# Token sums of squares ahead of four feed-forwards: one 512-column product of a high and a low part in place of a float32 product

## The chip, the cores and the metric

The kernel runs on one core of one Trainium2 chip. The metric is the device time of one launch in microseconds (us), and the reported number is the median of several runs. Before the change it is 1018.36 us (three runs, 1017.70 to 1018.63).

Engines are named as the profile names them: PE is TensorE (PEld its weight loads), DVE is VectorE, ACT is ScalarE, POOL is GpSimd, SP is SyncE, which only starts DMAs here.

## The reference

The input x is 256 tokens by 1024 features in float32, and the trunk has two layers. Each layer is feed-forward, mixer, feed-forward, with a root-mean-square norm ahead of every part:

```
def rms_norm(x, g):
    xf = x.astype(jnp.float32)
    y = xf * lax.rsqrt(jnp.mean(xf * xf, axis=-1, keepdims=True) + NORM_EPS)
    return (y * g.astype(jnp.float32)).astype(x.dtype)

def swiglu(h, w_in, w_out):
    gate, up = jnp.split(h @ w_in, 2, axis=-1)
    return (jax.nn.silu(gate) * up) @ w_out

for i in range(DEPTH):                       # DEPTH = 2
    x = x + 0.5 * swiglu(rms_norm(x, ffn1_norm[i]), ffn1_w_in[i], ffn1_w_out[i])
    hm = rms_norm(x, mix_norm[i])
    # layer 0: retention; layer 1: sliding-window attention over one shared K/V
    x = x + mixer(hm)
    x = x + 0.5 * swiglu(rms_norm(x, ffn2_norm[i]), ffn2_w_in[i], ffn2_w_out[i])
    if i == 0:
        k_sh, v_sh = shared_kv(x, kv_norm, kv_w, k_norm)
```

There are six norms of x, numbered m = 0 to 5: feed-forward, retention, feed-forward, feed-forward, attention, feed-forward. The change touches the four ahead of feed-forwards, m = 0, 2, 3 and 5. What it changes is how the sum of x*x over the 1024 features is formed for each token.

## The kernel before

**Layout.** x lies transposed: 128 partitions by 8 tiles (DT) by 256 tokens (T), 1024 features in all. A float32 weight of a projection is loaded to `stage`, ScalarE copies it to `w_hi` in the type float32r, and VectorE writes the rest, `stage - w_hi`, to `w_lo` (the helper `split`). The activations are split alike: `h[:, kt, 0:256]` holds the high and `h[:, kt, 256:512]` the low part. One `weight_block` on TensorE is a 512-column product `w_hi` x (high and low) and a 256-column product `w_lo` x high. The two halves of the PSUM bank are later added by ScalarE (copy of the right half) and VectorE (`add_halves_of`).

**Stages.** The program is one pass: feed-forward 0, retention, feed-forward 1, feed-forward 2 (with the shared K/V in it), attention, feed-forward 3. In a feed-forward, `in_group(f, g)` on TensorE computes four 128-column output blocks from two units of weights (`part` 0 and 1), four feature tiles `kt` in each. Even groups write PSUM banks 0 to 3 and odd groups banks 4 to 7. Eleven groups are followed by `out_tile`, one for each of the 8 tiles of x. The norm is not applied to h ahead of the product: h is x times gain, and the token's factor `r_row` multiplies the output of the group (`scale_of`, line 718). So TensorE starts the first group before the sum of squares is known.

**The sums of squares.** For m = 0 ScalarE squares all of x and VectorE adds the eight tiles in three steps (`first_sums`, lines 1077 to 1079). For later m GpSimd does it (`square_sum`): as each tile of x becomes final it squares it (line 1128) and adds it to `sq_sum` (line 1131). What is left is 128 partitions by 256 tokens. `norm_sum(m)` on TensorE multiplies it by a matrix of ones in float32, which puts the sum over all partitions into every row of a 256-column stretch of one bank. VectorE reads it (`token_sums`, line 668) into `n_v` and takes the inverse square root in nine steps (`token_scale`). For m = 3 two products of 2 columns also give the sums as columns, which the shared K/V uses.

**Order around the change.** The order of every engine is written out by hand; no scheduler moves anything. `norm_sum` stands in group 0 after `kt == 5` for m = 2 and 3, and in group 1 after `kt == 4` for m = 0 and 5 (LATE_NORMS), where it also waits until VectorE has read group 0's banks (`in_free`), since it writes bank 3. Engines wait for each other through semaphores that count. `lo_ready` counts units whose `w_lo` is written. TensorE waits for it ahead of each part of a group. On VectorE the order at the program's start is: eight quarters of units 0 and 1, unit 2 in halves, `first_sums`, `split(3)`, and then `first_groups` with `add_halves_of(0)`, `split(4)`, `token_sums`, `split(5)`, `token_scale`.

## Time and profile before

| what | value |
|---|---|
| median of three runs | 1018.36 us |
| the three runs | 1017.70, 1018.36, 1018.63 us |
| span of the profiled execution, first to last instruction | 1017.0 us |
| PE busy | 1012.4 us (5922 matmul instructions) |
| DVE busy | 780.5 us (874) |
| ACT busy | 496.9 us (536) |
| POOL busy | 95.8 us (91) |
| DMA | 185.31 MB, mean 182 GB/s |

No time of its own is given for the profiled execution beside its span. The median of the runs lies 1.4 us above the span, and that is taken as what lies around it (start and end of a launch). A busy PE is not PE at its peak: matmuls overlap, so what one costs is read from the distance between the starts of two neighbours and not from its own duration. A float32 product appears as two records of 256 columns. The lines 648 (`split` on VectorE) and 333 (`split` on ScalarE) are helpers that run 190 times each. Line 1159 is the helper through which nearly every matmul goes, so its rows are told apart by their operands.

### The profile page before, as it was taken

How to read it: one execution, taken by the hardware profiler on the slowest of the kernel's cores; microseconds unless marked ns; L12 is line 12 of the kernel's file. 1: busy time of each engine (PE TensorE's matmuls, PEld its weight loads, DVE VectorE, ACT ScalarE, POOL GpSimd, SP SyncE). 2: the span in 40 equal slices, each digit the busy share in tenths (PEclk: the TensorE clock that was granted, in tenths of full speed). 3: DMA queues.
4: the chain of work that ended last, by engine and by line, in shares of the span. 5: the costliest groups of instructions: out<-in, count | busy, mean ns of one | idle time of the engine just before them, and what ended most of it. 6: DMA issues, size and time to landing. Idle time of an engine off the chain costs nothing.

```text
span 1017.0 us, 15837 instructions
## 1 busy us (share of the span) xinstructions
PE 1012.4 (100%) x5922; PEld 885.6 (87%) x5922; DVE 780.5 (77%) x874; ACT 496.9 (49%) x536; POOL 95.8 (9%) x91
## 2 busy tenths in 40 slices
PE   9999999999999999999999999999999999999998
PEld 8888888888888888888888888888887898888888
DVE  7988867787797787777767787787778977877743
ACT  7455435544443364455444454465447944554432
POOL 0000013101100151000014100000210041000000
PEclk9999999999999999999999999999999999999999
DMA  9665456652652454554455645545563345544451
GB/s 351 237 233 180 142 175 219 249 194 103 215 191 103 187 184 154 204 203 167 148 186 201 248 165 189 192 145 171 183 239 121 104 161 193 207 166 167 156 193 63
DMA packets 32295, 185.31 MB, mean 182 GB/s; under 512 B 3840, under 2 KB 6400, under 8 KB 16128
## 3 DMA queue, kind: packets, MB, share of 16 engines
q1 hardware_dynamic: 31968, 184.64, 51.1%
q8 instruction: 23, 0.38, 0.1%
q10 hardware_dynamic: 288, 0.16, 0.1%
q14 instruction: 16, 0.13, 0.1%
HBM read 183.73 MB, written 1.05 MB: 182 GB/s over the span
## 4 chain that ended last, share of the span: by engine, by line
PE 99%; ACT 0%; POOL 0%; issue 0%; DVE 0%; DVEq 0%; POOLq 0%; ACTq 0%
PE ps L1159 98%; PE ps L1460 1%; POOL y_sq L1145 0%; PE ps L1427 0%; ACT w_hi L333 0%; ACT y_sq L493 0%; POOL sq_sum L1149 0%; ACT gate L471 0%; PE ps L1419 0%; DVE x L813 0%; DVE ones L1086 0%; POOLq L1142 0%; POOLq L1148 0%; ACT tmp L464 0%; DVEq L1085 0%
## 5 line engine op out<-in xcount | busy, mean ns | idle before, releaser
L1159 PE MATMUL ps<-h,w_hi 128*128 128x512 f32 x1664 | 580.8, 395 | 0.0
L1159 PE MATMUL ps<-h,w_lo 128*128 128x256 f32 x1664 | 462.2, 278 | 0.0
L648 DVE TENSOR_TENSOR w_lo<-stage,w_hi 128x2048 fp32r<-128x2048 f32 (+1 forms) x190 | 397.1, 2099 | 32.5 <-ACT w_hi L333 32.3
L1159 PEld LDWEIGHTS ps<-h,w_hi 128*128 128x128 f32 x1664 | 312.3, 188 | 71.6 <-issue 0.2
L333 ACT ACTIVATE w_hi<-stage 128x2048 fp32r<-128x2048 f32 (+1 forms) x190 | 326.8, 1728 | 6.3 <-PE ps L1159 5.5
L1159 PEld LDWEIGHTS ps<-h,w_lo 128*128 128x128 f32 x1664 | 313.0, 188 | 0.5
L1159 PE MATMUL ps<-act_t,w_hi 128*128 128x512 f32 (+1 forms) x726 | 244.8, 387 | 0.0
L1159 PE MATMUL ps<-act_t,w_lo 128*128 128x256 f32 x704 | 195.9, 278 | 0.0
L1159 PEld LDWEIGHTS ps<-act_t,w_hi 128*128 128x128 f32 x726 | 134.7, 188 | 29.5
L365 ACT ACTIVATE tmp<-ps 128x1024 f32<-128x1024 f32 x44 | 45.1, 1025 | 195.1 <-PE ps L1159 195.1
L1159 PEld LDWEIGHTS ps<-act_t,w_lo 128*128 128x128 f32 x704 | 132.5, 188 | 0.0
L712 DVE TENSOR_TENSOR tmp<-ps,tmp 128x1024 f32<-128x1024 f32 x44 | 53.8, 1223 | 70.4 <-ACT tmp L365 70.4
L398 ACT ACTIVATE tmp<-ps 128x256 f32<-128x256 f32 x39 | 14.9, 381 | 120.0 <-PE ps L1159 120.0
L1159 PE MATMUL ps<-w_hi,h 128*128 128x512 f32 x192 | 60.4, 395 | 0.0
L758 DVE SCALAR_TENSOR_TENSOR tmp<-ps,tmp 128x256 f32<-128x256 f32 x39 | 16.4, 422 | 54.2 <-ACT tmp L398 54.1
L370 ACT ACTIVATE tmp<-tmp 128x512 f32<-128x512 f32 x44 | 27.9, 633 | 58.3 <-DVE tmp L718 58.3
L718 DVE TENSOR_TENSOR tmp<-tmp,r_row 128x1024 f32<-128x1024 f32 x44 | 53.9, 1225 | 1.5
L1131 POOL TENSOR_TENSOR sq_sum<-sq_sum,sq 128x256 f32<-128x256 f32 x35 | 48.4, 1384 | 2.7
L1159 PE MATMUL ps<-y_t,w_hi 128*128 128x512 f32 x128 | 45.3, 399 | 0.0
L1122 POOL TENSOR_TENSOR sq_sum<-x 128x256 f32<-128x256 f32 x5 | 3.1, 615 | 444.5 <-DVE x L760 381.4
L1128 POOL TENSOR_TENSOR sq<-x 128x256 f32 x35 | 31.0, 885 | 130.8 <-DVE x L760 128.9
L1159 PEld LDWEIGHTS ps<-w_hi,h 128*128 128x128 f32 x192 | 35.1, 188 | 7.8 <-issue 0.7
(158 smaller groups left out, 738.6 us busy)
## 6 DMA issues: line engine op xcount, KB each, us to landing
stage<-w_in_dram SPq DMA_DIRECT2D x85, 1024.0 KB, 4.8
stage<-w_out_dram SPq DMA_DIRECT2D x64, 704.0 KB, 4.1
stage<-w_ret_dram SPq DMA_DIRECT2D x24, 1024.0 KB, 4.9
stage<-w_ret_out_dram SPq DMA_DIRECT2D x8, 1024.0 KB, 4.8
stage<-w_q_dram SPq DMA_DIRECT2D x4, 1024.0 KB, 5.7
stage<-w_o_dram SPq DMA_DIRECT2D x4, 1024.0 KB, 4.8
stage<-w_in_dram SPq DMA_DIRECT2D x8, 256.0 KB, 4.4
stage<-w_in_dram SPq DMA_DIRECT2D x2, 512.0 KB, 6.0
```

The costliest lines, as they stand in the source:

```text
L333: nc.scalar.activation(w_hi[:, s, 0:n], stage[:, s, 0:n], ACT.Copy).then_inc(hi_ready, 1)
L365: nc.scalar.activation(t, ps[:, 4 * (g % 2):4 * (g % 2) + 4, T:2 * T], ACT.Copy).then_inc(in_lo_half, 1)
L370: nc.scalar.activation(tmp[:, g % 2, 0:512], tmp[:, g % 2, 0:512], ACT.Silu).then_inc(in_silu, 1)
L398: nc.scalar.activation(tmp[:, d % 2, 0:T], ps[:, bank, T:2 * T], ACT.Copy, scale=scale).then_inc(out_lo_half, 1)
L648: nc.vector.tensor_tensor(w_lo[:, s, 0:n], stage[:, s, 0:n], w_hi[:, s, 0:n].bitcast(F32), ALU.subtract).then_inc(lo_ready, 1)
L712: nc.vector.tensor_tensor(t, ps[:, 4 * (g % 2):4 * (g % 2) + 4, 0:T], t, ALU.add).then_inc(in_free, 1)
L718: nc.vector.tensor_tensor(t, t, same(r_row[:], 4), ALU.mult).then_inc(in_scaled, 1)
L758: chain.step(nc.vector.scalar_tensor_tensor(t, ps[:, bank, 0:T], scale, t, ALU.mult, ALU.add))
L1128: nc.gpsimd.tensor_tensor(sq[:].rearrange("p (a n) -> p a n", a=1), x[:, ds(i + 1, 1), :], x[:, ds(i + 1, 1), :], ALU.mult).then_inc(sq_do ...
L1131: nc.gpsimd.tensor_tensor(sq_sum[:], sq_sum[:], sq[:], ALU.add).then_inc(sum_added, 1)
L1159: return nc.tensor.matmul(out_, w, x_, start=start, stop=stop)
L1460: last = nc.tensor.transpose(ps[:, P_T_BANKS[e][r], q * P:(q + 1) * P], s[:, h0 + head, kb * P:(kb + 1) * P], ident[:])
```

## The change

For m = 0, 2, 3 and 5 the sum of squares is split into a high part in float32r and the rest, both 256 columns, side by side in `sq_parts`. One product with the matrix of ones in float32r, 512 columns wide, replaces the float32 product of 256 columns. The two 256-column halves of the bank are added as VectorE reads them: `token_sums` is two instructions where it was one. The split is made by GpSimd for m = 2, 3 and 5 (a copy and a subtraction after the last addition; the last round of the loop is written out) and by VectorE for m = 0 (two instructions at the end of `first_sums`). The two column products of m = 3 move to bank 6 and read `sq_all`. The retention's and the attention's sums and the per-head sums stay as they are.

```diff
@@ -184,6 +184,8 @@
     n_t = at("n_t", [P, T], F32, misc + 22528)
     sq_sum = at("sq_sum", [P, T], F32, misc + 23552)
     sq = at("sq", [P, T], F32, misc + 24576)
+    sq_parts = at("sq_parts", [P, 2 * T], F32R, misc + 23552)
+    sq_all = at("sq_all", [P, T], F32, misc + 27200)
     gain = at("gain", [P, (NORMS + 1) * DT], F32, misc + 25600)
     sinks = at("sinks", [P, HEADS_Q], F32, misc + 25824)
     r_col = at("r_col", [P, 4], F32, misc + 25888)
@@ -193,7 +195,7 @@
     sm = at("sm", [P, len(SOFTMAXES), 5, CH], F32, misc + 26240)
 
     ps = nc.alloc_psum_tensor("ps", [P, 8, 512], F32)
-    SUM, FIRST_SUM = 7, 3
+    SUM, FIRST_SUM, COLUMNS = 7, 3, 6
 
     sem = nc.alloc_semaphore
     landed = [sem(f"landed{s}") for s in range(SLOTS)]
@@ -208,6 +210,7 @@
     ones_ready, tables_ready = sem("ones_ready"), sem("tables_ready")
     x_squared = sem("x_squared")
     sq_done, sum_added = sem("sq_done"), sem("sum_added")
+    sq_hi, sq_lo, half_added = sem("sq_hi"), sem("sq_lo"), sem("half_added")
     sum_done, sum_read, r_ready = sem("sum_done"), sem("sum_read"), sem("r_ready")
     h_hi, h_lo = sem("h_hi"), sem("h_lo")
     in_lo_half, in_free = sem("in_lo_half"), sem("in_free")
@@ -665,10 +668,16 @@
 
 
                 dve.wait_ge(sum_done, sums_before(m) + 1)
-                ins = nc.vector.tensor_scalar(n_v[:], ps[:, FIRST_SUM if m in LATE_NORMS else SUM, 0:T], V_SCALE / D, V_SCALE * EPS,
-                                              ALU.mult, ALU.add)
-                if m == 3:
-                    ins = nc.vector.tensor_scalar(col_v[:], ps[:, SUM, T:T + 4], V_SCALE / D, V_SCALE * EPS, ALU.mult, ALU.add)
+                bank = FIRST_SUM if m in LATE_NORMS else SUM
+                ins = nc.vector.tensor_scalar(n_v[:], ps[:, bank, 0:T], V_SCALE / D, V_SCALE * EPS, ALU.mult, ALU.add)
+                if m in FFN_NORM:
+                    ins.then_inc(half_added, 1)
+                    if m == 3:
+                        nc.vector.tensor_scalar(col_v[:], ps[:, COLUMNS, 0:4], V_SCALE / D, V_SCALE * EPS, ALU.mult,
+                                                ALU.add)
+                    dve.wait_ge(half_added, FFN_NORM.index(m) + 1)
+                    ins = nc.vector.scalar_tensor_tensor(n_v[:], ps[:, bank, T:2 * T], V_SCALE / D, n_v[:], ALU.mult,
+                                                         ALU.add)
                 ins.then_inc(sum_read, 1)
 
             def token_scale(m):
@@ -1076,7 +1085,12 @@
                 half = x_sq[:, 0:4, :]
                 chain.step(nc.vector.tensor_tensor(half, half, x_sq[:, 4:8, :], ALU.add))
                 chain.step(nc.vector.tensor_tensor(x_sq[:, 0:2, :], x_sq[:, 0:2, :], x_sq[:, 2:4, :], ALU.add))
-                nc.vector.tensor_tensor(sq_sum[:], x_sq[:, 0, :], x_sq[:, 1, :], ALU.add).then_inc(sum_added, DT)
+                nc.vector.tensor_tensor(sq_all[:], x_sq[:, 0, :], x_sq[:, 1, :], ALU.add).then_inc(sum_added, DT)
+                dve.wait_ge(sum_added, DT)
+                nc.vector.tensor_scalar(sq_parts[:, 0:T], sq_all[:], 1.0, None, ALU.mult).then_inc(sq_hi, 1)
+                dve.wait_ge(sq_hi, 1)
+                nc.vector.tensor_tensor(sq_parts[:, T:2 * T], sq_all[:], sq_parts[:, 0:T].bitcast(F32),
+                                        ALU.subtract).then_inc(sq_lo, 1)
 
             dve.sem_inc(in_free, CREDIT)
             dve.sem_inc(a_ready, CREDIT)
@@ -1120,7 +1134,8 @@
                 pool.wait_ge(sum_done, sums_before(m))
                 pool.wait_ge(x_done, CREDIT + DT * (m - 1) + 1)
                 nc.gpsimd.tensor_tensor(sq_sum[:], x[:, 0, :], x[:, 0, :], ALU.mult).then_inc(sum_added, 1)
-                with pool.Fori(0, DT - 1) as i:
+                parts = m in FFN_NORM
+                with pool.Fori(0, DT - 2 if parts else DT - 1) as i:
 
                     pool.wait_ge(sum_added, added_for(m) - DT + 1 + i)
 
@@ -1129,6 +1144,18 @@
                                             x[:, ds(i + 1, 1), :], ALU.mult).then_inc(sq_done, 1)
                     pool.wait_ge(sq_done, (DT - 1) * (m - 1) + 1 + i)
                     nc.gpsimd.tensor_tensor(sq_sum[:], sq_sum[:], sq[:], ALU.add).then_inc(sum_added, 1)
+                if parts:
+                    pool.wait_ge(sum_added, added_for(m) - 1)
+                    pool.wait_ge(x_done, CREDIT + DT * m)
+                    nc.gpsimd.tensor_tensor(sq[:], x[:, DT - 1, :], x[:, DT - 1, :], ALU.mult).then_inc(sq_done, 1)
+                    pool.wait_ge(sq_done, (DT - 1) * m)
+                    nc.gpsimd.tensor_tensor(sq_all[:], sq_sum[:], sq[:], ALU.add).then_inc(sum_added, 1)
+                    n = FFN_NORM.index(m)
+                    pool.wait_ge(sum_added, added_for(m))
+                    nc.gpsimd.tensor_copy(sq_parts[:, 0:T], sq_all[:]).then_inc(sq_hi, 1)
+                    pool.wait_ge(sq_hi, n + 1)
+                    nc.gpsimd.tensor_tensor(sq_parts[:, T:2 * T], sq_all[:], sq_parts[:, 0:T].bitcast(F32),
+                                            ALU.subtract).then_inc(sq_lo, 1)
 
 
             pool.wait_ge(rope_loaded, 32)
@@ -1183,11 +1210,16 @@
 
                 pe.wait_ge(sum_added, added_for(m))
                 if m in (3, ATT):
+                    bank, first, sums = (COLUMNS, 0, sq_all) if m == 3 else (SUM, T, sq_sum)
                     for t in range(2):
-                        last = matmul(ps[:, SUM, T + 2 * t:T + 2 * t + 2], sq_sum[:, t * P:(t + 1) * P],
+                        last = matmul(ps[:, bank, first + 2 * t:first + 2 * t + 2], sums[:, t * P:(t + 1) * P],
                                       ones[:, 0:2], True, True)
-                if m != ATT:
-                    last = matmul(ps[:, FIRST_SUM if m in LATE_NORMS else SUM, 0:T], ones[:], sq_sum[:], True, True)
+                if m in FFN_NORM:
+                    pe.wait_ge(sq_lo, FFN_NORM.index(m) + 1)
+                    last = matmul(ps[:, FIRST_SUM if m in LATE_NORMS else SUM, :], ones[:].bitcast(F32R), sq_parts[:],
+                                  True, True)
+                elif m == RET:
+                    last = matmul(ps[:, SUM, 0:T], ones[:], sq_sum[:], True, True)
                 last.then_inc(sum_done, 1)
 
             def first_blocks(kt):
```

**VectorE at the program's start**, from the end of `first_sums` through `first_groups`. `x_sq` holds the squares of x, `n_v` the token sums read from PSUM, `r_row` the token factor. Before:

```order
L1078 TENSOR_TENSOR x_sq<-x_sq 128x512
L1079 TENSOR_TENSOR sq_sum<-x_sq 128x256
L648 TENSOR_TENSOR w_lo<-stage,w_hi 128x2048
L712 TENSOR_TENSOR tmp<-ps,tmp 128x1024
L648 TENSOR_TENSOR w_lo<-stage,w_hi 128x2048
L668 TENSOR_SCALAR n_v<-ps 128x256
L648 TENSOR_TENSOR w_lo<-stage,w_hi 128x2048
L653 TENSOR_SCALAR r_row<-n_v 128x256
```

And of the change:

```order
L1087 TENSOR_TENSOR x_sq<-x_sq 128x512
L1088 TENSOR_TENSOR sq_all<-x_sq 128x256
L1090 TENSOR_SCALAR sq_parts<-sq_all 128x256
L1092 TENSOR_TENSOR sq_parts<-sq_all,sq_parts 128x256
L651 TENSOR_TENSOR w_lo<-stage,w_hi 128x2048
L721 TENSOR_TENSOR tmp<-ps,tmp 128x1024
L651 TENSOR_TENSOR w_lo<-stage,w_hi 128x2048
L672 TENSOR_SCALAR n_v<-ps 128x256
L679 SCALAR_TENSOR_TENSOR n_v<-ps,n_v 128x256
L651 TENSOR_TENSOR w_lo<-stage,w_hi 128x2048
L656 TENSOR_SCALAR r_row<-n_v 128x256
```

Two instructions now stand ahead of the split of unit 3 (the first `w_lo` row) and of `add_halves_of(0)` (the `tmp<-ps,tmp` row), and a third one stands ahead of the split of unit 5.

**GpSimd at the end of the sum for m = 2.** The rows REGISTER_ALU, ISA and COMPARE_AND_BRANCH are the loop's own. Before:

```order
L1128 TENSOR_TENSOR sq<-x 128x256
L1130 REGISTER_ALU
L1131 TENSOR_TENSOR sq_sum<-sq_sum,sq 128x256
L1123 REGISTER_ALU
L1123 COMPARE_AND_BRANCH
L1122 TENSOR_TENSOR sq_sum<-x 128x256
```

And of the change:

```order
L1143 TENSOR_TENSOR sq<-x 128x256
L1145 REGISTER_ALU
L1146 TENSOR_TENSOR sq_sum<-sq_sum,sq 128x256
L1138 REGISTER_ALU
L1138 COMPARE_AND_BRANCH
L1150 TENSOR_TENSOR sq<-x 128x256
L1152 TENSOR_TENSOR sq_all<-sq_sum,sq 128x256
L1155 CAST sq_parts<-sq_all 128x256
L1157 TENSOR_TENSOR sq_parts<-sq_all,sq_parts 128x256
L1136 TENSOR_TENSOR sq_sum<-x 128x256
```

The last of the eight tiles is taken out of the loop, and a copy (CAST) and a subtraction follow its addition; TensorE's product waits for the subtraction where it waited for the addition. The last row of each is the start of the next norm's sum. On TensorE nothing moves: in each of the four places one row `ps<-sq_sum,ones 128x256` becomes `ps<-sq_parts,ones 128x512`.

## Rows read from the trace of the kernel before

**Rows 1.** The page, the chain that ended last, by engine.
```profile
PE 99%; ACT 0%; POOL 0%; issue 0%; DVE 0%; DVEq 0%; POOLq 0%; ACTq 0%
```

**Rows 2.** The page, granted TensorE clock in 40 slices, in tenths.
```profile
PEclk9999999999999999999999999999999999999999
```

**Rows 3.** Timeline of PE around m = 0; start, duration, engine, line, out<-in, form.
```profile
24.31 0.40 PE L1159 MATMUL ps<-h,w_hi 128*128 128x512 f32 x1
24.55 0.28 PE L1159 MATMUL ps<-h,w_lo 128*128 128x256 f32 x1
24.68 0.59 PE L1159 MATMUL ps<-sq_sum,ones 128*128 128x256 f32 x2
...
25.34 0.28 PE L1159 MATMUL ps<-h,w_lo 128*128 128x256 f32 x1
```

**Rows 4.** Timeline of PE around the sum for m = 3.
```profile
578.32 0.50 PE L1159 MATMUL ps<-ones,sq_sum 128*128 128x2 f32 x4
578.68 0.68 PE L1159 MATMUL ps<-sq_sum,ones 128*128 128x256 f32 x2
...
579.43 0.28 PE L1159 MATMUL ps<-h,w_lo 128*128 128x256 f32 x1
```

**Rows 5.** Timeline of DVE, program's start.
```profile
19.94 0.42 DVE L1079 TENSOR_TENSOR sq_sum<-x_sq 128x256 f32<-128x256 f32 x1
20.28 2.28 DVE L648 TENSOR_TENSOR w_lo<-stage,w_hi 128x2048 fp32r<-128x2048 f32 x1
22.48 1.22 DVE L712 TENSOR_TENSOR tmp<-ps,tmp 128x1024 f32<-128x1024 f32 x1
...
28.35 0.28 DVE L653 TENSOR_SCALAR r_row<-n_v 128x256 int32<-128x256 int32 x1
28.67 0.71 DVE L659 TENSOR_TENSOR n_t<-r_row 128x256 f32<-128x256 f32 x1
```

**Rows 6.** Timeline of PEld and of PE, first block that needs unit 3.
```profile
23.14 0.19 PEld L1159 LDWEIGHTS ps<-h,w_hi 128*128 128x128 f32 x1
...
23.25 0.40 PE L1159 MATMUL ps<-h,w_hi 128*128 128x512 f32 x1
```

**Rows 7.** Timeline of POOL and of PEld, a wait of TensorE in the retention.
```profile
344.21 0.74 POOL L1149 TENSOR_TENSOR sq_sum<-y_sq 128x256 f32<-128x256 f32 x1 [0.16 <-POOL y_sq L1145]
...
345.00 0.30 PEld L1159 LDWEIGHTS ps<-sq_sum,ones 128*128 128x128 f32 x2 [0.40 <-POOL sq_sum L1149]
```

**Rows 8.** Timeline of POOL and DVE, end of the sum for m = 2.
```profile
390.25 0.81 POOL L1131 TENSOR_TENSOR sq_sum<-sq_sum,sq 128x256 f32<-128x256 f32 x1
...
391.74 2.29 DVE L648 TENSOR_TENSOR w_lo<-stage,w_hi 128x2048 fp32r<-128x2048 f32 x1 [1.29 <-ACT w_hi L333]
```

**Rows 9.** Timeline of POOL and DVE, a tile of m = 1.
```profile
146.25 0.61 POOL L1128 TENSOR_TENSOR sq<-x 128x256 f32 x1 [7.03 <-DVE x L760]
146.33 2.02 DVE L648 TENSOR_TENSOR w_lo<-stage,w_hi 128x1408 fp32r<-128x1408 f32 x1 [0.28 <-ACT w_hi L333]
146.94 2.00 POOL L1131 TENSOR_TENSOR sq_sum<-sq_sum,sq 128x256 f32<-128x256 f32 x1
```

**Rows 10.** Timeline of PE, the sums for m = 2 and 5.
```profile
394.85 0.59 PE L1159 MATMUL ps<-sq_sum,ones 128*128 128x256 f32 x2
...
848.17 0.59 PE L1159 MATMUL ps<-sq_sum,ones 128*128 128x256 f32 x2
```

**Rows 11.** Timeline of POOL, last additions for m = 3 and 5.
```profile
572.43 0.80 POOL L1131 TENSOR_TENSOR sq_sum<-sq_sum,sq 128x256 f32<-128x256 f32 x1
...
842.28 0.74 POOL L1131 TENSOR_TENSOR sq_sum<-sq_sum,sq 128x256 f32<-128x256 f32 x1
```

**Rows 12.** Timeline of DVE, reads of the sums for m = 2, 3 and 5.
```profile
395.48 0.42 DVE L668 TENSOR_SCALAR n_v<-ps 128x256 f32<-128x256 f32 x1 [1.45 <-PE ps L1159]
...
579.40 0.42 DVE L668 TENSOR_SCALAR n_v<-ps 128x256 f32<-128x256 f32 x1 [0.98 <-PE ps L1159]
...
848.80 0.42 DVE L668 TENSOR_SCALAR n_v<-ps 128x256 f32<-128x256 f32 x1 [2.33 <-PE ps L1159]
```

## The prediction

> **What bounds the kernel now.** I read first the chain that ended last, by engine [rows 1]: TensorE holds 99% of the span, and every other engine rounds to nothing. The reader is to see that only two things can move the end: time that TensorE no longer spends on a product, and time that it newly waits. Then the granted clock [rows 2]: full speed, which is 2.4 GHz, in every slice. Then the timeline of TensorE around each of the four sums [rows 3, 4, 10], for what a sum costs in the stream, and last the timelines of VectorE and GpSimd around the same places [rows 5, 8, 9, 11, 12], for how early each of TensorE's waits is met today.
>
> **Term 1, the product.** TensorE's matmuls overlap, so I take distances between starts. The 512-column float32r product of weights and h starts at 24.31 and the next matmul at 24.55: it costs 0.24 us [rows 3]. The sum for m = 0 starts at 24.68, and the second matmul after it at 25.34. Between them lie the sum and one such 512-column product, so the sum costs 25.34 - 24.68 - 0.24 = 0.42 us. The starts at m = 2 and 5 look the same [rows 10], and I use 0.42 for all three. For m = 3 the sum follows the two column products, and the same reckoning gives 579.43 - 578.68 - 0.24 = 0.51 us [rows 4]. The new product has the shape and type of the 0.24 us one. The saving is 3 x (0.42 - 0.24) + (0.51 - 0.24) = 0.81 us. Bounds: nothing, if the new product cost what the float32 one does; 1.77 us if it cost nothing at all (3 x 0.42 + 0.51), which is already under the 2.0 us that are 0.2% of the time. I take 0.81, since the row is of the same form. The column products only change bank and source: no cost.
>
> **Term 2, VectorE at the start (m = 0).** Two instructions now stand between the last addition and the split of unit 3. The addition ends at 19.94 + 0.42 = 20.36, and the split starts at 20.28, 0.08 before that end, as it depends on nothing there [rows 5]. The new ones depend on each other: a gap of 0.04 (28.35 + 0.28 to 28.67), a TENSOR_SCALAR of 256 columns in SBUF (0.28, the row at 28.35), 0.04 again, and a subtraction of 256 columns (0.42, as the addition). The split then starts at 20.36 + 0.04 + 0.28 + 0.04 + 0.42 - 0.08 = 21.06, which is 0.78 later, and ends at 23.34 in place of 22.56.
>
> Who waits for it: TensorE's first block of unit 3, whose weight load starts at 23.14 and whose product at 23.25 [rows 6]. From the end of what releases it to a load takes 0.05 us (344.21 + 0.74 = 344.95 to 345.00) [rows 7], so the split must end by 23.09. Today there are 0.53 us to spare. With 0.78 more TensorE waits 0.25 us. The shift is bounded by 0.66 (no gaps and overlap kept: 0.28 + 0.42, less 0.04) and 1.0 (two instructions of 0.42 with gaps of 0.08), so the wait by 0.13 and 0.47; two as slow as the 0.71 at 28.67 would shift it by 1.4 and make the wait 0.9. I take 0.25.
>
> Queued behind the two on VectorE is also `add_halves_of(0)`. It ends at 22.48 + 1.22 = 23.70 today, and the sum's product waits for it: its load starts near 24.57, so 24.52 is the limit, 0.82 us later. The shift of 0.78 fits, barely, and TensorE's own 0.25 gives more room. Past that come the split of unit 4, `token_sums`, and the split of unit 5. TensorE wants bank 3 read and unit 4 ready for group 2, three feature tiles after the sum: 12 blocks of some 0.36 us (24.31 to 24.68 [rows 3]), thus 24.68 + 0.42 + 4.3 = 29.4. `token_sums` begins today after `add_halves_of(0)` and one split of 2.28, near 25.9; with 0.78 and two instructions (0.88) it ends near 27.6. That is covered by 1.8 us.
>
> **Term 3, the second read.** `token_sums` grows by one instruction of 0.42 and a gap of 0.04 at each of four places. It reads PSUM like the first one, which takes 0.42 [rows 12]. For m = 2 the read ends at 395.48 + 0.42 = 395.90 today; with 0.46 more, and the sum done 0.18 earlier, 396.2. TensorE's group 1 waits for it and starts eight blocks after the sum, 394.85 + 0.24 + 8 x 0.36 = 398.0: covered by 1.8 us. For m = 3 it is 579.40 + 0.42 + 0.46 and some 0.15 for the columns, 580.4, against 581.8. For m = 0 and 5 group 2 follows 12 blocks after. The later steps (inverse root, scaling, banks handed back) come 0.46 later, but group 2 is the first to need group 0's banks when m is 2 or 3, a whole group of 32 blocks (11 us) further on. Cost: nothing; with that cover gone, 0.46 at each place, 1.8 us in all.
>
> **Term 4, GpSimd's copy and subtraction (m = 2, 3, 5).** TensorE's product now waits for the subtraction. No copy on GpSimd is in the trace. The nearest row is x*x of 256 columns, 0.61 us (one source), and the addition of two sources, 0.81 [rows 8, 9]. For m = 2: the addition ends at 391.06; after a gap of 0.08 (146.86 to 146.94) the copy runs from 391.14 to 391.75 if it takes 0.61. The subtraction could start at 391.83. But VectorE's split of a unit comes at 391.74 [rows 8], and rows 9 show what such a meeting does: the addition that is due at 146.94, while a split is under way since 146.33, takes 2.00 in place of 0.81 and ends 0.59 after the split's end at 148.35. So the two take turns. The split gets the turn at 391.75, ends near 394.04, and the subtraction ends near 394.63. TensorE's load for the sum stands at about 394.74 (0.11 ahead of 394.85 [rows 10]) and needs the release by 394.69: met with 0.06 us to spare, so I take 0. If the copy takes 0.81, everything moves 0.2 and TensorE waits 0.14. If it takes under about 0.5, the subtraction goes ahead of the split and ends near 392.4. The split is then pushed back by up to 0.8, which VectorE's idle 1.45 ahead of its read [rows 12] covers.
>
> The Trainium skill (SBUF — State Buffer, the section on the two sides of SBUF) says that VectorE and GpSimd share a pair of ports under an exclusive lock held for a whole instruction. The trace agrees: 2.00 against 0.81 in rows 9. Without that rule the subtraction would end at 392.6, and the sum would be the same. The Trainium skill (GPSIMD Engine Reference, Engine selection) says that one-input work on GpSimd runs at roughly line rate and that two-input work is about twice as slow as on VectorE. No run here shows a copy; by that rule it would be shorter than 0.61, the subtraction would go first, and rival C below would be gone, with the sum unchanged.
>
> For m = 3 the addition ends at 573.23 [rows 11]. Even behind a whole split of 2.29 the subtraction ends at about 573.92 + 2.29 + 0.59 = 576.8, against 578.68. For m = 5 it ends at 843.02, and the same gives 846.6 against 848.17. Both are covered, by 1.8 and 1.4 us. GpSimd has nothing else in its queue until the next norm. No DMA is added or moved; the slot of unit 3 is handed back 0.8 us later, and its next content is needed a group and a half later.
>
> **The sum.** -0.81 + 0.25 + 0 + 0 = -0.56 us. The profiled span is 1017.0 us, and the median of the runs lies 1.4 above it: 1017.0 - 0.56 + 1.4 = 1017.8 us, 0.05% under 1018.36.
>
> **The rivals.**
>
> A, nothing waits at the start. If VectorE's two instructions shifted the split by under 0.53, the whole 0.81 would stay: 1018.36 - 0.81 = 1017.55 us. Against it: the subtraction alone has a 0.42 row. For it: only that the order of starts overlaps by 0.08.
>
> B, the product gains nothing, so that the change does not do what it says: 512 columns could cost 0.42 as 256 float32 columns do, with the ones as weights. Then only the wait of term 2 is left: 1018.36 + 0.25 = 1018.6 us. Against it is the 0.24 of the same form [rows 3]. For it: nothing but that the weights are another tensor.
>
> C, slower than before through GpSimd's tail at m = 2. If the copy takes c, at least 0.61, it holds VectorE's split back until 391.14 + c. The split ends 2.29 later and the subtraction 0.59 after that, at 394.02 + c, so TensorE waits c - 0.67. The gain is used up from c = 1.23 on. With the 2.00 of the addition that had to wait [rows 9] it is 1.33: 1017.8 + 1.33 = 1019.1 us. To lose more than 0.2% against before the copy would have to take 3.3 us. Against it: every row on GpSimd of this size that had to wait for nobody lies at 0.61 to 0.81.
>
> D, the clock. A wait could make TensorE's clock fall to 1.2 GHz, where each block takes twice as long: after 3 us of lost time this is slower by over 0.2%, about 1021. Against it: the wait at 345.00 [rows 7] left the granted clock at full speed [rows 2], and that one is as long as the one I expect.
>
> **How the numbers follow.** The forecast has 0.68, A 0.10, B 0.10, C 0.08, D and what I don't see 0.04. The predicted time is the forecast's, 1017.8. Its own terms span 1017.3 (less wait) to 1018.2 (a wait of 0.47 at the start and 0.14 at m = 2), and the median of a few runs scatters by some 0.4 us, as the three of before do. The range 1017.0 to 1018.9 holds the forecast, A and B, and most of C. About 0.2% (2.0 us) is what a measurement of this kernel can tell from no change. No case gains that much, as four free sums would give 1.77: faster 0.02 for what I don't see. Slower by 0.2% needs D or the far end of C: 0.04. Within: 0.94.
>
> **What would show it.** In the changed kernel's profile the product for each sum should stand 0.24 before the next start, at four places. TensorE's load for the first block of unit 3 should name VectorE's split as what released it, with a wait of about 0.25 and the split ending near 23.34. The subtraction on GpSimd for m = 2 should take about 2.8 from its due time, behind a split, and end just ahead of TensorE's sum; or it precedes the split, which then shows over 2.29. VectorE's second read should be 0.42 and nobody should wait for it. I am wrong if the sums' distances stay at 0.42, if TensorE waits at m = 2 or at the start of group 1 or 2, or if PEclk shows a slice under 9.

## The result: slower by 0.67%, and the profile after

| kernel | executions | median | lowest to highest | ratio to before, 95% interval |
|---|---|---|---|---|
| before | 6 | 1018.31 us | 1017.70 to 1018.63 | |
| changed | 6 | 1025.60 us | 1020.87 to 1027.76 | 1.0067 [1.0057, 1.0078] |

The prediction was 1017.8 us in a range of 1017.0 to 1018.9. It was wrong in the size, the sign and the range. A second thing is new: the kernel before scatters by 1 us here (and between 1017.3 and 1019.2 in its 103 executions beside the experiments), the changed one by 7. The profiled execution of the changed kernel is the one of 1024.23 us, with a span of 1022.3.

The page of the changed kernel, chain and granted clock. They answer to [rows 1, 2] and show nothing new.

```profile
PE 99%; ACT 0%; POOL 0%; issue 0%; DVE 0%; DVEq 0%; POOLq 0%; ACTq 0%
```
```profile
PEclk9999999999999999999999999999999999999999
```

Timeline of PE of the changed kernel around the sum for m = 2, with its neighbours, and on into the pairs right behind it (answers to [rows 3, 10]; start, duration). "..." stands for rows left out.

```profile
393.76 0.27 PE L1186 MATMUL ps<-h,w_lo 128*128 128x256 f32 x1
...
394.10 0.28 PE L1186 MATMUL ps<-h,w_lo 128*128 128x256 f32 x1
394.22 0.39 PE L1186 MATMUL ps<-sq_parts,ones 128*128 128x512 f32 x1
394.45 0.39 PE L1186 MATMUL ps<-h,w_hi 128*128 128x512 f32 x1
394.67 0.28 PE L1186 MATMUL ps<-h,w_lo 128*128 128x256 f32 x1
...
395.02 0.28 PE L1186 MATMUL ps<-h,w_lo 128*128 128x256 f32 x1
...
395.38 0.28 PE L1186 MATMUL ps<-h,w_lo 128*128 128x256 f32 x1
...
395.74 0.28 PE L1186 MATMUL ps<-h,w_lo 128*128 128x256 f32 x1
...
396.08 0.28 PE L1186 MATMUL ps<-h,w_lo 128*128 128x256 f32 x1
```

The sum costs 394.45 - 394.22 = 0.23 us and nobody waits. What differs is what comes behind it. From one w_lo row to the next is one pair of products: ahead of the sum 393.76 to 394.10 is 0.34, behind it the distances from 395.02 on are 0.36, 0.36 and 0.34. One such distance, rounded to 0.01, says little. The next w_lo rows of before and after show it over a whole stretch: from the sum for m = 2 to the columns for m = 3 lie the same 527 pairs in each. Timeline of PE, before:

```profile
395.51 0.28 PE L1159 MATMUL ps<-h,w_lo 128*128 128x256 f32 x1
...
578.20 0.28 PE L1159 MATMUL ps<-h,w_lo 128*128 128x256 f32 x1
```

The changed kernel starts its stretch at 394.67 (above) and ends it here, ahead of the columns and the sum for m = 3:

```profile
580.88 0.28 PE L1186 MATMUL ps<-h,w_lo 128*128 128x256 f32 x1
581.00 0.50 PE L1186 MATMUL ps<-ones,sq_all 128*128 128x2 f32 x4
581.37 0.48 PE L1186 MATMUL ps<-sq_parts,ones 128*128 128x512 f32 x1
581.68 0.39 PE L1186 MATMUL ps<-h,w_hi 128*128 128x512 f32 x1
```

182.69 / 527 = 0.3467 us for a pair before, 186.21 / 527 = 0.3533 after: 0.0067 more, 527 times. No row in the stretch shows a wait. The view by windows shows it as a count: w_lo products of PE in fixed windows (window, length, busy time and count, granted clock, DMA share, GB/s). Before:

```profile
30.00:190.00 160.00, 127.84 (x462) 1.00 0.55 191
...
400.00:570.00 170.00, 137.34 (x491) 1.00 0.52 180
590.00:735.00 145.00, 115.89 (x419) 1.00 0.52 183
860.00:1000.00 140.00, 111.88 (x405) 1.00 0.51 177
```

After, the same windows, which lie in feed-forwards 0, 1, 2 and 3:

```profile
30.00:190.00 160.00, 129.34 (x462) 1.00 0.55 193
...
400.00:570.00 170.00, 135.15 (x482) 1.00 0.52 179
590.00:735.00 145.00, 115.32 (x411) 1.00 0.51 176
860.00:1000.00 140.00, 113.07 (x405) 1.00 0.53 180
```

In feed-forwards 1 and 2 the same time holds 482 pairs in place of 491, and 411 in place of 419, at a granted clock of 1.00 (2.4 GHz) in both. I call 0.3467 the quick cadence and 0.3533 the slow one; no third was seen over a long stretch of pairs. Most of the extra time sits in the 512-column product: averaged over a stretch of 15 us its start-to-start distance is 0.230 to 0.232 quick and 0.236 to 0.237 slow, and that of the 256-column product 0.115 to 0.117 in both.

The same window rows hold one thing more. Busy time over count is the mean length of a w_lo record, and in quick windows it has two values: 127.84 / 462 = 0.2767 us in feed-forward 0 of before, 129.34 / 462 = 0.2800 after. So the quick cadence comes in two forms. In the one of 0.2800 all w_lo rows are 0.28 long, in the one of 0.2767 rows of 0.27 and 0.28 take turns (393.76 and 394.10 above). The slow one repeats by threes, 0.36, 0.36, 0.34. The form matters below.

With the two cadences the books close. Pairs at the slow cadence that were quick before: 527 in feed-forward 1 and 459 in feed-forward 2, at 0.0066: 3.5 + 3.0 us. The other way round: 111 pairs between 355 and 394, slow in the profile of before and quick after: -0.7. The four products: -0.8. TensorE's wait at the start: 0.2. The program's start itself ran 0.2 later (the w_lo row at 9.36 stands at 9.55). Together 5.4, against 1022.3 - 1017.0 = 5.3.

### The profile page after: what moved, and what is told of

It is laid out like the page before. It is cut to its first block, busy times and chain, and to the rows that moved or that the text cites. A ratio compares the mean times of both kernels' runs of the same rounds, so it can differ in the third digit from the quotient of the medians.

```text
span 1022.3 us, 15827 instructions
## 1 busy us (share of the span) xinstructions
PE 1017.7 (100%) x5918; PEld 888.7 (87%) x5918; DVE 783.5 (77%) x880; ACT 496.8 (49%) x536; POOL 99.3 (10%) x97
## 4 chain that ended last, share of the span: by engine, by line
PE 99%; ACT 0%; POOL 0%; issue 0%; DVE 0%; DVEq 0%; POOLq 0%; ACTq 0%
PE ps L1186 98%; PE ps L1492 1%; POOL y_sq L1172 0%; PE ps L1459 0%; ACT w_hi L336 0%; ACT y_sq L496 0%; POOL sq_sum L1176 0%; ACT gate L474 0%; PE ps L1451 0%; DVE x L822 0%; DVE ones L1100 0%; POOLq L1169 0%; POOLq L1175 0%; ACT tmp L467 0%; DVEq L1099 0%
## 5 line engine op out<-in xcount | busy, mean ns | idle before, releaser
L1146 POOL TENSOR_TENSOR sq_sum<-sq_sum,sq 128x256 f32<-128x256 f32 x32 | 46.1, 1440 | 2.5
```

The costliest lines, as they stand in the source:

```text
L1146: nc.gpsimd.tensor_tensor(sq_sum[:], sq_sum[:], sq[:], ALU.add).then_inc(sum_added, 1)
```

## The experiments

The kernel before was timed beside each set. The cadence of each feed-forward is read from the one profiled execution; for the others it is inferred from the groups of their times, since one slow feed-forward adds 3.2 (f0, 491 pairs), 3.5 (f1, 527), 3.0 (f2, 459) or 3.1 us (f3, 475). No kernel leaves out any of the computation; "extra" products are overwritten or never read. q is quick, s slow; the number of executions stands in brackets.

Theory S, formed on the two traces: the stream of pairs keeps a cadence, and what TensorE does at a sum sets it. Its rival N: the new waits and the other engines' work slow the stream. Theories P, F, O and L in the later expectations are versions of S on what it is at a sum that sets it.

| run | what | executions, us | ratio, 95% interval | f0 f1 f2 f3 in the profile |
|---|---|---|---|---|
| before | | 1017.3 to 1019.2 (103) | | q q q q |
| changed | | 1020.9; 1024.2 to 1025.7 (3); 1027.6, 1027.8 | 1.0067 [1.0057, 1.0078] | q s s q |
| e1 | float32 sums back | 1018.1 to 1019.4 (11) | 1.0007 [0.9998, 1.0016] | q q q q |
| e2 | float32 for m = 2 only | 1018.2 to 1019.0 (4); 1021.1 to 1022.2 (4); 1023.8 to 1024.2 (4) | 1.0035 [1.0022, 1.0047] | q q q q |
| e3 | before + one 512 | 1018.4 to 1019.2 (5); 1021.1 to 1022.0 (6) | 1.0023 [1.0014, 1.0032] | q q q q |
| e4 | + small float32 | 1024.9 to 1028.9 (5) | 1.0085 [1.0072, 1.0098] | s s q s |
| e5 | sums as 256 + 256 | 1027.7 to 1031.2 (4) | 1.0111 [1.0096, 1.0127] | s s s s |
| e6 | before + 512 + 512 | 1017.9 to 1019.9 (11) | 1.0006 [0.9997, 1.0015] | q q q q |
| e7 | before + 512 + 256 | 1018.1 to 1019.3 (11) | 1.0000 [0.9991, 1.0010] | q q q q |
| e8 | before + one 256 | 1021.0 to 1021.9 (7) | 1.0029 [1.0017, 1.0040] | q q s q |
| e9 | m = 5 only | 1017.2 to 1019.1 (11) | 0.9997 [0.9988, 1.0005] | q q q q |
| e10 | m = 0 only | 1018.1 to 1019.6 (6); 1021.1 to 1022.7 (6) | 1.0019 [1.0009, 1.0029] | s q q q |
| e11 | m = 2 only | 1020.6 to 1021.1 (6); 1022.1 to 1022.3 (3) | 1.0029 [1.0019, 1.0038] | q s q q |
| e12 | + long float32 | 1022.7 to 1023.7 (4); 1026.6, 1026.9 | 1.0059 [1.0044, 1.0074] | q q s q |
| e13 | m = 3 only | 1018.1 to 1018.8 (5); 1020.4 to 1020.9 (6) | 1.0015 [1.0006, 1.0024] | q q q q |
| e14 | m = 5 only, 256 + 256 | 1020.4 to 1021.7 (6) | 1.0032 [1.0020, 1.0044] | q q q s |
| e15 | m = 5 only, 512 + 256 | 1020.6 to 1021.7 (7) | 1.0029 [1.0018, 1.0040] | q q q s |
| e16 | m = 5 only, 512 + 256 + 256 | 1017.5 to 1019.2 (10); 1021.5 | 1.0007 [0.9998, 1.0016] | q q q q |

**e1, float32 products back, everything else of the change kept.** In `norm_sum`, for all four m; the second read stays and is multiplied by 0 (its lines, and the `if m in (0, 2, 3, 5)` around these, are left out here):

```diff
-                    last = matmul(ps[:, FIRST_SUM if m in LATE_NORMS else SUM, :], ones[:].bitcast(F32R), sq_parts[:],
-                                  True, True)
+                        last = matmul(ps[:, FIRST_SUM if m in LATE_NORMS else SUM, 0:T], ones[:], sq_all[:], True, True)
```

> The changed kernel with TensorE's product back in float32 (256 columns of sq_all) at all four sums. The split into high and low parts, TensorE's wait for it and VectorE's second read stay (the second read is multiplied by 0). Theory S (stream): a pair of products of weights and h costs 0.3467 us or 0.3533 us depending on how the stream was entered, a float32 product leaves it at 0.3467, and the float32r product for m = 2 left it at 0.3533 through two feed-forwards. Then this kernel is back at 1018 to 1019 us, with the two cadences where the kernel before has them, and its runs scatter by under 1 us. Rival N: the added waits, the GpSimd and VectorE instructions or the other code slow the stream. Then the time stays near 1024 to 1026.

It came back to 1018.69 us, all eleven in one group. So the waits, GpSimd's and VectorE's new work and the new code together cost 0.65 us by the medians (1018.69 against 1018.04; by the interval between -0.2 and 1.6), and the rest of the 7 us comes with the type and shape of TensorE's product. Rival N is out as the cause of the 7 us.

**e2, the same for m = 2 alone.** The condition `m == 2` on both edits of e1.

> The changed kernel with the float32 product back for m = 2 alone. Theory S: feed-forward 1 runs at 0.3467 again, some 180 us or 527 pairs, 3.5 us less than the profiled execution of the changed kernel. Whether feed-forward 2 follows depends on what the float32r product for m = 3 does to a stream that comes in at 0.3467: if it leaves it, the time is about 1018; if it flips it, about 1021. Rival N: near 1025 as the changed kernel.

Three groups of four executions, some 3 us apart, which fits none, one or two feed-forwards slow. In the profiled execution, one of the fastest group, all four are quick. So the float32r products leave it to chance, and nothing here shows which feed-forward is slow in the other groups. The median, 1021.61, describes none of the groups but the middle one.

**e3, the kernel before with one extra product.** In `in_group`, after the pairs of the seventh tile:

```diff
+                        if g == 0 and kt == 6 and m == 2:
+                            for _ in range(1):
+                                matmul(ps[:, 6, :], ones[:].bitcast(F32R), h[:, 0, :], True, True)
```

> The kernel before with one extra 512-column float32r product of ones and h in feed-forward 1, after the float32 sum for m = 2 (in group 0 after the seventh feature tile); its result is overwritten unread. No wait, no other engine. Theory S: if a float32r product of its own between the pairs flips the cadence, feed-forward 1 runs at 0.3533 until the float32 products of m = 3: 527 x 0.0066 = 3.5 us, about 1022. Rival N (only waits and other engines matter): 0.23 us more, 1018.6.

No wait and no other engine was touched, and 6 of 11 executions are 2.7 us slower for 0.23 us of work. The profiled execution is of the faster group, with all four feed-forwards quick. The theory had the wrong feed-forward, perhaps: the distance of the groups, 2.7, fits feed-forward 2 (3.0) better than 1 (3.5), and e8 shows that place plainly.

**e4, a short float32 product behind each sum.**

```diff
+                    matmul(ps[:, 2 if m in LATE_NORMS else 5, 0:2], ones[:], ones[:, 0:2], True, True)
```

> The changed kernel with a 2-column float32 product of ones right behind each of the four float32r sum products. It costs 0.1 to 0.2 us at each place. Theory S: it brings the stream back to 0.3467 each time, and the time is 1018 to 1018.5 with little scatter. If what counts is the size of the float32 product and not its kind, or rival N holds, it stays at 1024 to 1027.

Refuted as far as the kind alone goes: three feed-forwards slow, the time up. A float32 product of 2 columns does not bring the quick cadence back.

**e5, the sum as two products of 256 columns, added in PSUM, one read.**

```diff
-                    last = matmul(ps[:, FIRST_SUM if m in LATE_NORMS else SUM, :], ones[:].bitcast(F32R), sq_parts[:],
-                                  True, True)
+                    row = ps[:, FIRST_SUM if m in LATE_NORMS else SUM, 0:T]
+                    matmul(row, ones[:].bitcast(F32R), sq_parts[:, 0:T], True, False)
+                    last = matmul(row, ones[:].bitcast(F32R), sq_parts[:, T:2 * T], False, True)
```

> The changed kernel with the 512-column float32r product at each of the four sums cut in two float32r products of 256 columns, high part and low part, added up in one stretch of PSUM; VectorE reads once as in the kernel before. TensorE's own cost is about the same 0.23 us. What the executions so far show is that a lone 512-column float32r product leaves each following feed-forward at 0.3467 or 0.3533 us for a pair, differently from one execution to the next. Theory P (place of 512-column products): two 512-column products in a row, sum and then weights, are what shifts the stream; two of 256 then keep it, the time is 1017.5 to 1018 and scatters by under 1.5 us. Theory F (only the long float32 product brings the stream back): anything else leaves the state to chance, and the time scatters from 1018 to 1028 as for the changed kernel, in steps of about 3.2 us.

The slowest of all, with every feed-forward slow in the profile, although TensorE has no more to do than in the changed kernel and VectorE one instruction less for each sum. Theory P is refuted. Theory F gave 1018 to 1028, and three of the four executions lie above that, at 1031.0 to 1031.2.

**e6, e7 and e8: other extra products at the place of e3** (`matmul(ps[:, 6, 0:c], ones[:].bitcast(F32R), h[:, 0, 0:c], True, True)` with c = 512 and 512, 512 and 256, and 256).

> The kernel before with two extra 512-column float32r products in feed-forward 1 behind the sum for m = 2, where e3 had one. Theory P: three in a row, the state of feed-forward 1 is left to chance as in e3, 1018.3 or 1021.8. If what counts is an even or odd number of products (two weight buffers in turn), two keep it: all executions at 1018.5. Theory F: left to chance, two groups of times 3.3 us apart.

> The kernel before with an extra pair, a 512-column and a 256-column float32r product, at the same place, so that long and short products go on in turn. Theory P and the even number both say that it keeps the stream: all executions at 1018.4. Theory F as far as it says that any extra product disturbs: two groups of times, 1018.4 and 1021.8.

> The kernel before with one extra 256-column float32r product at the same place. Theory P: no two long ones in a row, all executions near 1018.2. Even or odd number: left to chance or flipped, a group near 1021.7. Theory F: two groups 3.3 us apart.

Two extra products keep every execution where it was, whatever their length; a single one of 256 columns moves all seven. That speaks against P and F, and for odd and even. In e8's profile feed-forward 1, where the product stands, stays quick, and it is feed-forward 2 that is slow, behind the unchanged float32 products for m = 3. Windows of e8, w_lo products of PE in feed-forwards 1 and 2, against x491 and x419 before:

```profile
400.00:570.00 170.00, 135.84 (x491) 1.00 0.52 180
590.00:735.00 145.00, 115.28 (x411) 1.00 0.52 180
```

And of e6:

```profile
400.00:570.00 170.00, 135.85 (x491) 1.00 0.51 179
590.00:735.00 145.00, 117.18 (x419) 1.00 0.54 183
```

So the stream carries something that its cadence doesn't show, and a float32 sum doesn't always end quick. A part of it shows in the form: in feed-forward 1 both e8 and e6 have w_lo records of 0.2767 us (135.84 and 135.85 / 491), where before has 0.2797 (137.34 / 491). The extra products changed the form at once and the cadence not at all. Behind the same float32 products for m = 3, e6 is quick (0.2797) and e8 slow, so the form at the entry doesn't settle it either.

**e9, e10, e11 and e13: the change at one norm alone.** A tuple `PARTS` in place of `FFN_NORM` in the changed functions, and `first_sums` as before where 0 is not in it.

> The change for m = 5 alone (GpSimd's split, the 512-column float32r product, the second read); m = 0, 2 and 3 as in the kernel before. Only feed-forward 3 follows, 475 pairs. The theory (the state of the pair stream is carried on; the float32 product of 256 columns brings it to 0.3467, a float32r product does not by itself): the executions fall in two groups, one 0.2 under the kernel before, near 1018.1, and one 475 x 0.0066 = 3.1 us above it, near 1021.2, or all in one of them. Rival N (it is the waits and the other engines' work): one group, evenly a part of the 7 us, near 1020.

> The change for m = 0 alone, with VectorE's split at the program's start. Theory: one group at the time before less 0.19 plus TensorE's wait for the split of unit 3 (0.17 in the changed kernel's profile), 1018.3, and one with feed-forward 0 at 0.3533, 491 x 0.0066 = 3.2 us above, 1021.6. The float32 sum for m = 1 ends it, so nothing is carried further. Rival N: one group.

> The change for m = 2 alone. Theory: groups at 1018.1 (nothing slow), 1021.6 (feed-forward 1 at 0.3533, 527 pairs, 3.5 us), 1021.1 (feed-forward 2, 459 pairs, 3.0 us, if the products of m = 3 pass a changed stream on, as after the lone 256-column product of e8) and 1024.6 (both). Rival N: one group near 1020.

> The change for m = 3 alone. Theory O (odd and even: an odd number of float32r products turns the state of the stream over, an even one keeps it): feed-forward 2 enters at 0.3467, gets one float32r product, and leaves at 0.3533 in all executions: 1018.1 + 459 x 0.0066 = 1021.1 us. Theory L (each place has its own outcome, set by lengths and distances): either one group.

The change at m = 5 never slows the kernel, at m = 2 it always does, at m = 0 and m = 3 in about half of the executions (6 of 12 and 6 of 11). e11's profile, of its lower group, has feed-forward 1 at x482 and the others quick; what the upper group, 1.4 us above, has in addition is not shown. For e13 theory O expected all executions slow, and five of eleven were not.

**e12, a float32 product as long as that of the kernel before, behind each sum.** As e4 with `[:, 0:T]` and `sq_all`.

> The changed kernel with a float32 product of 256 columns, unread, right behind the float32r product at each of the four sums, where e4 had a float32 product of 2 columns. It costs 4 x 0.42 = 1.7 us in itself. Theory: the long float32 product is what brings the stream to 0.3467, whatever stood ahead of it: 1017.8 + 1.7 = 1019.5 us in one group, under the changed kernel itself although TensorE does more. If the count of products decides (the sum now adds one to the float32 kernel's), some feed-forwards stay slow: 1022 to 1029 in groups.

Not one group. Feed-forward 1 is quick, feed-forward 2 slow (x411 in its window), and two executions have one more slow. The long float32 product alone isn't the cure either; in e1, without the float32r product ahead of it, all eleven executions stayed in the fast group.

**e14, e15 and e16: m = 5 alone, with 2, 2 and 3 products in place of 1.** Nothing lies downstream but feed-forward 3, and the stream came in slow in every profile.

```diff
-                    last = matmul(ps[:, FIRST_SUM if m in LATE_NORMS else SUM, :], ones[:].bitcast(F32R), sq_parts[:],
-                                  True, True)
+                    matmul(ps[:, FIRST_SUM, 0:T], ones[:].bitcast(F32R), sq_parts[:, 0:T], True, True)
+                    last = matmul(ps[:, FIRST_SUM, T:2 * T], ones[:].bitcast(F32R), sq_parts[:, T:2 * T], True, True)
```

e15 and e16 keep the 512-column product and put one or two of these behind it: `matmul(ps[:, 2, 0:T], ones[:].bitcast(F32R), sq_parts[:, 0:T], True, True)`.

> The change for m = 5 alone with two float32r products of 256 columns, one for each half of the bank, in place of the one of 512. The stream enters at 0.3533. Theory O: an even number keeps it, feed-forward 3 is slow in all executions, 1018.3 + 475 x 0.0066 = 1021.4 us. Theory L: as e9, which has the same columns, 1018.3.

> The change for m = 5 alone with one unread 256-column float32r product behind the 512-column one: an even number, and a long and a short one like every pair around it. Theory O: stays at 0.3533, 1021.4 us. Theory L: nothing to say beforehand; 1018.4 would speak against O.

> The change for m = 5 alone with two unread 256-column float32r products behind the 512-column one: an odd number again. Theory O: turned over to 0.3467 as by the one product of e9, 0.23 us more than e9: 1018.5 us in all executions. With e15 at 1021.4 TensorE would do more work in less time.

Theory O fits 34 of 35 executions: one product quick (11 of 11, e9, which was known when O was formed), two slow (6 of 6 and 7 of 7), three quick (10 of 11). The last three it forecast. e14 and e9 push the same 512 columns through the same weights, and lie 3.2 us apart. Timeline of PE of e9 at the sum:

```profile
847.41 0.28 PE L1184 MATMUL ps<-h,w_lo 128*128 128x256 f32 x1
847.53 0.40 PE L1184 MATMUL ps<-sq_parts,ones 128*128 128x512 f32 x1
847.77 0.40 PE L1184 MATMUL ps<-h,w_hi 128*128 128x512 f32 x1
848.01 0.28 PE L1184 MATMUL ps<-h,w_lo 128*128 128x256 f32 x1
```

And of e14:

```profile
847.96 0.28 PE L1184 MATMUL ps<-h,w_lo 128*128 128x256 f32 x1
848.07 0.40 PE L1184 MATMUL ps<-sq_parts,ones 128*128 128x256 f32 x2
848.31 0.40 PE L1184 MATMUL ps<-h,w_hi 128*128 128x512 f32 x1
848.56 0.28 PE L1184 MATMUL ps<-h,w_lo 128*128 128x256 f32 x1
```

From w_lo to w_lo both take 0.60 us. At the sum nothing tells them apart; the windows in feed-forward 3 do. e9, then e14:

```profile
860.00:1000.00 140.00, 113.07 (x405) 1.00 0.50 177
```
```profile
860.00:1000.00 140.00, 111.30 (x397) 1.00 0.52 177
```

And e16, quick like e9 but in the other form (111.86 / 405 = 0.2762 us against 113.07 / 405 = 0.2792):

```profile
860.00:1000.00 140.00, 111.86 (x405) 1.00 0.51 176
```

**A wait moves the stream as well.** For m = 0 the load of the first block of unit 3 waits for VectorE's split, about 1.5 us ahead of the sum. Timeline of PE of e2, whose load waits 0.40 us there:

```profile
9.55 0.28 PE L1187 MATMUL ps<-h,w_lo 128*128 128x256 f32 x1
...
23.07 0.28 PE L1187 MATMUL ps<-h,w_lo 128*128 128x256 f32 x1
...
23.76 0.28 PE L1187 MATMUL ps<-h,w_lo 128*128 128x256 f32 x1
...
24.12 0.28 PE L1187 MATMUL ps<-h,w_lo 128*128 128x256 f32 x1
...
24.48 0.28 PE L1187 MATMUL ps<-h,w_lo 128*128 128x256 f32 x1
...
24.82 0.28 PE L1187 MATMUL ps<-h,w_lo 128*128 128x256 f32 x1
```

From 9.55 to 23.07 lie 39 pairs, 0.3467 each: quick. Behind the wait come 0.36, 0.36, 0.34: the slow repeat, though over three pairs only. Behind the sum the feed-forward is quick. In the changed kernel it goes the other way: the stream comes in slow, reads 0.35, 0.35, 0.34 (23.85, 24.20, 24.55, 24.89) behind a wait of 0.22, and is quick before the new product is reached.

**What stays open.** What state of TensorE it is that one matmul more or less, or a wait, changes, so that all that follow cost more or less. Odd and even fit the cadence in e6 and e7 and in e9 with e14 to e16, but a state of two turns is too small: in feed-forward 3 one product (e9) and three (e16) leave two forms of the quick cadence, and two leave the slow one. They don't explain why the lone product for m = 2 slows every execution while the one of e3 and e8 leaves its own feed-forward quick, nor e12, nor the halves of e10 and e13. For m = 0 the wait's length differs between profiles (0.22 us in the changed kernel, 0.40 in e2, 0.47 in e10, 1.36 in e4), which may be the source of chance; no run here ties it to the groups. Nor is the kernel before free of it: the pairs from 356 to 394 are slow in its profile (x108 w_lo products in that window) and quick in that of e9 (x110), with the same instructions up to there. No version here beats the kernel before beyond its interval; e9 comes nearest with 0.9997 [0.9988, 1.0005].

## Why the prediction was wrong, step by step

**Term 1 is the step that failed.** It priced a sum by its own stretch of the stream, and took the pairs behind it as unchanged. The product itself was near: 0.23 us for m = 0 and 2 and 0.24 for m = 5, where 0.24 was said, and for m = 3, right behind the column products, 0.31 (581.37 to 581.68 above), where 0.24 was said. But what stands at a sum also decides the cadence of the next 459 to 527 pairs: behind the float32 products they ran quick in every feed-forward of before and of e1, behind the new ones they ran slow in two of four. In the profiled execution that cost 6.5 us; over all four feed-forwards it is worth up to 12.8 us, 16 times the 0.81 of the term. The evidence lay in the trace of before. Timeline of PE, the first and last w_lo rows of the stretches ahead of and behind the sum for m = 0, whose inner ends, 24.55 and 25.34, stand in [rows 3]:

```profile
9.36 0.28 PE L1159 MATMUL ps<-h,w_lo 128*128 128x256 f32 x1
...
195.55 0.28 PE L1159 MATMUL ps<-h,w_lo 128*128 128x256 f32 x1
```

Ahead lie 43 pairs in 15.19 us, 0.3533 each, and behind it 491 in 170.21, 0.3467 each. At m = 2 and 5 it turns in the same way. I read one pair at each sum and never a stretch. My signs of being wrong looked only at the sums' distances, at waits and at the clock, and none of them appeared: the change was slower without any.

**Term 2 was right in place and near in size.** VectorE at the start, answers to [rows 5]:

```profile
20.04 0.43 DVE L1088 TENSOR_TENSOR sq_all<-x_sq 128x256 f32<-128x256 f32 x1
20.50 0.29 DVE L1090 TENSOR_SCALAR sq_parts<-sq_all 128x256 fp32r<-128x256 f32 x1
...
20.83 0.43 DVE L1092 TENSOR_TENSOR sq_parts<-sq_all,sq_parts 128x256 fp32r<-128x256 f32 x1
21.18 2.28 DVE L651 TENSOR_TENSOR w_lo<-stage,w_hi 128x2048 fp32r<-128x2048 f32 x1
```

The split ends at 23.46, 0.12 later than said since the stretch began 0.1 later. And TensorE's load for the first block of unit 3, answer to [rows 6]:

```profile
23.51 0.19 PEld L1186 LDWEIGHTS ps<-h,w_hi 128*128 128x128 f32 x1 [0.22 <-DVE w_lo L651]
```

It waits 0.22 against the 0.25 predicted, released by VectorE as said; the load moved from 23.14 to 23.51, of which 0.2 is the later start, so 0.17 is lost. That near hit is in part luck: the 0.53 us to spare was that of one execution. In e3, whose start is the code of before, the same load waits 0.55.

**Term 3 was right.** The second read takes 0.42 (VectorE, m = 2), and nobody waits:

```profile
394.65 0.42 DVE L672 TENSOR_SCALAR n_v<-ps 128x256 f32<-128x256 f32 x1
395.11 0.42 DVE L679 SCALAR_TENSOR_TENSOR n_v<-ps,n_v 128x256 f32<-128x256 f32 x1
```

**Term 4 was right in its result, by the other of its two branches.** The main branch, in which the split goes first, did not happen. GpSimd and VectorE of the changed kernel at m = 2, answers to [rows 8]:

```profile
390.28 0.83 POOL L1152 TENSOR_TENSOR sq_all<-sq_sum,sq 128x256 f32<-128x256 f32 x1
391.18 0.40 POOL L1155 CAST sq_parts<-sq_all 128x256 fp32r<-128x256 f32 x1
391.65 0.74 POOL L1157 TENSOR_TENSOR sq_parts<-sq_all,sq_parts 128x256 fp32r<-128x256 f32 x1
```
```profile
391.83 2.71 DVE L651 TENSOR_TENSOR w_lo<-stage,w_hi 128x2048 fp32r<-128x2048 f32 x1 [1.32 <-ACT w_hi L336]
```

The copy took 0.40 and not 0.61, so the subtraction was ahead of VectorE's split and ended at 392.39. The split paid instead: 2.71 in place of the 2.29 of [rows 8]. The Trainium skill (GPSIMD Engine Reference, Engine selection) had said that one-input work runs at roughly line rate. The trace agrees that it is the cheap kind: 0.40 for the copy against 0.61 for x*x and 0.83 for two sources, and 0.29 for VectorE's own copy (20.50 above). The Trainium skill's rule of the exclusive lock on the shared ports (SBUF — State Buffer, Who interferes with whom) is shown here from the other side, with VectorE as the one that loses 0.42.

**The rivals.** A: the wait came, so no. B: the product gained what it should, so no. C: the tail on GpSimd ended 1.8 us before TensorE's sum, so no. D, the clock: PEclk 1.00 in every window, so no, though its kind of harm, every later block dearer, was what happened, by 1.9% and not by 100%. D and all unseen causes together had 0.04. Also false was the argument that four free sums, 1.77 us, bound the change on the good side: the cadence is not in them, and the 111 pairs between 355 and 394 did go the good way, by 0.7.

**Two slips of the sum, without weight.** The lower end of its own terms, 1017.3, doesn't follow: with no wait at all it is 1018.36 - 0.81 = 1017.55. And the 1.4 between median and span is of two different executions: within one it is 1.9 (1024.23 against 1022.3).

## What to carry to other kernels

Where TensorE bounds a kernel, measure the distance between starts over a few hundred matmuls ahead of and behind each irregular product, in each stage; one row is too coarse for 2%, and a window's count is enough. A product that breaks a regular stream of matmuls is priced by what the stream does afterwards, which experiments with one more and two more idle products show quickly. When the executions of one kernel fall in groups some us apart, look for a stage with two speeds before explaining the median, and don't read a single profile as the kernel: for e2, e3 and e13 it showed the fastest group.

## What the runs showed of the hardware

- A stream of alternating 512- and 256-column float32r matmuls, each with its own weights, has two lasting cadences at the full clock of 2.4 GHz: 0.3467 and 0.3533 us for a pair, over hundreds of pairs and through loops. The quick one has two forms, with w_lo records of 0.277 or 0.280 us in the mean; the slow one repeats by three pairs, 0.36, 0.36, 0.34.
- Work in between moves it from one to the other. At m = 5 one float32r product left the quick one in 11 of 11 executions, two the slow one in 13 of 13, three the quick one in 10 of 11; two idle products more (e16) made the kernel 2.2 us faster than one more (e15).
- The sums as float32 products of 256 columns left the quick cadence in every feed-forward in the profiles of e1 and of the kernel before, but not for m = 3 in e8.
- A wait of TensorE for its weights can move the stream too: 0.40 us in e2, from 0.3467 to distances of 0.36, 0.36, 0.34.
- A copy of 128x256 float32 to float32r on GpSimd took 0.40 us.
